# A two-block transformer in one launch: the last block's 16 attention heads run as eight pairs, and the expert rows get rings of four buffers

## The reference, cut to what matters

```python
h = modulate(rms_norm(x, norm_attn), sh1, sc1)
x = x + g1 * hybrid_mixer(h, w_in, w_out, rel_bias)      # 16 causal heads of 64
h = modulate(rms_norm(x, norm_ffn), sh2, sc2)
x = x + g2 * peer_ffn(h, peer_wq, peer_subkeys, peer_u, peer_v)
return rms_norm(x, norm_final)
```

## Time and profile before

| what | value |
|---|---|
| median of 3 runs | 2196.6 us (2193.18 to 2200.11) |
| the profiled execution | 2197.04 us, its span 2195.8 us |
| busy: TensorE / VectorE / ScalarE / GpSimd | 1870.3 / 1365.4 / 783.3 / 891.7 us |
| first scores of the heads to end of the last `out2` half | 1270.1 to 1428.5 us |
| first gather issued, last gather issued | 1468.1 us, 2170.2 us |
| gathered from the two tables | 268.47 MB on the software queue |

### The profile page before, as it was taken

The page is one execution under the profiler, slowest core; times in us unless marked ns, Lnnn a source line. Parts: engine busy times, 40 slices in busy tenths (PEclk is TensorE's granted clock), DMA queues, the critical chain, the costliest instruction groups (busy, mean ns, idle before and its releaser), DMA issues.

```text
span 2195.8 us, 29808 instructions
## 1 busy us (share of the span) xinstructions
PE 1870.3 (85%) x11372; PEld 1514.3 (69%) x11372; DVE 1365.4 (62%) x2217; ACT 783.3 (36%) x1235; POOL 891.7 (41%) x858
## 2 busy tenths in 40 slices
PE   7999978999899988778999888878777777777786
PEld 7999967999899987668999776676333233333332
DVE  6766764765476455657664574268878886444444
ACT  5443343543344334444443354332322323111111
POOL 5511630002552365340005012025566776677774
PEclk9999998999999999989999898789988988999999
DMA  7775634555566554334556244148899999999996
GB/s 237 220 274 183 205 112 140 167 191 198 176 212 201 196 162 156 130 106 136 173 199 202 80 141 144 49 133 326 325 390 384 404 389 381 375 410 409 410 410 275
DMA packets 248228, 516.47 MB, mean 235 GB/s; under 512 B 16017, under 2 KB 157634, under 8 KB 248130
## 3 DMA queue, kind: packets, MB, share of 16 engines
q0 software_dynamic: 83280, 302.06, 36.4%
q1 hardware_dynamic: 164178, 211.92, 28.9%
q10 hardware_dynamic: 672, 1.18, 0.2%
HBM read 509.86 MB, written 5.26 MB: 235 GB/s over the span
## 4 chain that ended last, share of the span: by engine, by line
PE 31%; POOL 24%; issue 23%; DVE 13%; DMA 5%; ACT 4%; POOLq 0%; ACTq 0%; SPq 0%; DVEq 0%
POOL GU L566 8%; POOL GV L566 8%; PE PX L593 5%; PE PX L594 5%; PE PX L595 5%; PE P L593 3%; PE P L594 3%; PE P L595 3%; POOL adaW L486 3%; DVE WL L1393 2%; DMA adaW<-in_w_ada 2%; DVE GU L1922 2%; ACT WH L1031 2%; POOL adaW L488 2%; DMA GU<-in_peer_u,M 2%
## 5 line engine op out<-in xcount | busy, mean ns | idle before, releaser
L966 PE MATMUL P<-GV,M 128*128 128x512 f32 x1024 | 516.0, 663 | 155.7 <-ACT M L1331 140.8
L593 PE MATMUL PX<-hTh,WH 128*128 128x256 f32 x1928 | 559.0, 290 | 34.3 <-DVE WL L1393 15.5
L594 PE MATMUL PX<-hTl,WH 128*128 128x256 f32 x1928 | 552.2, 286 | 0.0
L595 PE MATMUL PX<-hTh,WL 128*128 128x256 f32 x1928 | 551.9, 286 | 0.0
L966 PEld LDWEIGHTS P<-GV,M 128*128 128x128 f32 x1024 | 212.1, 212 | 454.3 <-issue 325.3
L1393 DVE TENSOR_TENSOR WL<-WR,WH 128x2048 fp32r<-128x2048 f32 x134 | 319.5, 2385 | 265.9 <-ACT WH L1031 265.7
L1922 DVE CUSTOM_DVE_ANT_0 GU<-GU,PX 128x1024 f32<-128x1024 f32 x256 | 297.4, 1218 | 205.1 <-DMA GU<-in_peer_u,M 185.6
L593 PEld LDWEIGHTS PX<-hTh,WH 128*128 128x128 f32 x1928 | 377.1, 196 | 42.4 <-DVE WL L1393 21.1
L1031 ACT ACTIVATE WH<-WR 128x2048 fp32r<-128x2048 f32 x134 | 255.8, 1909 | 350.8 <-PE P L595 191.3
L594 PEld LDWEIGHTS PX<-hTl,WH 128*128 128x128 f32 x1928 | 377.3, 196 | 0.9 <-issue 0.7
L595 PEld LDWEIGHTS PX<-hTh,WL 128*128 128x128 f32 x1928 | 376.9, 195 | 0.0
(11 more groups left out here) (279 smaller groups left out, 2266.3 us busy)
## 6 DMA issues: line engine op xcount, KB each, us to landing
WR<-in_ffn_w_up SPq DMA_DIRECT2D x88, 1024.0 KB, 7.5
WR<-in_ffn_w_down SPq DMA_DIRECT2D x44, 1024.0 KB, 6.5
adaW<-in_w_ada POOLq DMA_DIRECT2D x48, 512.0 KB, 4.9
WR<-in_diff_w_in SPq DMA_DIRECT2D x14, 1024.0 KB, 6.4
WR<-in_w_in SPq DMA_DIRECT2D x13, 1024.0 KB, 6.8
WR<-in_mem_w_kv SPq DMA_DIRECT2D x8, 1024.0 KB, 7.2
WR<-in_peer_wq SPq DMA_DIRECT2D x8, 1024.0 KB, 8.9
WR<-in_pool_w_in SPq DMA_DIRECT2D x6, 1024.0 KB, 6.5
```

The source lines that it names most:

```text
L593: mm(o, wh, xh, start=first, stop=False, skip_group_check=skip)
L594: mm(o, wh, xl, start=False, stop=False, skip_group_check=skip)
L595: return mm(o, wl, xh, start=False, stop=last, skip_group_check=skip)
L966: last = mm(P[2 * t + q][:], diag[:, g, i], GV[:, g, i, q * 512:q * 512 + 512], start=first and i == 0, stop=False, skip_group_check=True)
```

## The change

In the attention of the last block two heads form a pair. A pair's scores leave out keys 128 to 255 of the first query tile, which the mask hides: per head 128 + 256 = 384 columns in place of 512 (`W2`), 768 for the pair. Logits, maxima, exponentials, scaling and the copy of the transposes work on 768 columns per pair; there are six transposes in place of eight, and the second v product has 128 columns. `topk` reads only the first 128 keys for the first tile. The `in2` projections move to the PSUM banks P0 and P1, the pairs use P4 to P7 and start each turn with their v product. Turns 0 to 3 carry two `in2` halves each, turn 4 one; turns 5, 6 and 8 an `out2` half. Scores of pairs 0 to 7 wait until the projections that they need are copied (`bank_free`).

In the expert stage groups 0 to 5 use two buffers and later groups four: the two added ones lie where weights and splits lay, so group 6's u rows wait until all `wq` halves are used. GpSimd's order becomes u(n+1) before v(n). The last group's v rows have a semaphore each. The g2 row is built ahead of group 6 and not between the tiles; tile 0's final sum is done during tile 1; the closing matmuls with zeros (line 998) go.

```diff
-    OUT2_SLOTS = {11: 0, 12: 1, 15: 2}
+    IN2_SLOTS = {0: [5, 6], 1: [7, 8], 2: [9, 10], 3: [11, 12], 4: [13]}
+    OUT2_SLOTS = {5: 0, 6: 1, 8: 2}
...
+        def gather_u(n):
+            call = ALL_CALLS.index((n // GROUPS, n % GROUPS * NG // 16))
+            pool.wait_ge(S["index_ready"], call + 1)
+            if user_before(n) is not None:
+                pool.wait_ge(S["dots_ready"], user_before(n) + 1)
+            if n == EARLY:
+                pool.wait_ge(S["half_used"], len(half_of))
+            gathers(rows_u(n), ub, [u_landed[ring(n)]] * NG, n)
+
+        def gather_v(n):
+            if user_before(n) is not None:
+                pool.wait_ge(S["v_used"], user_before(n) + 1)
+            gathers(rows_v(n), vb, last_landed if n == 2 * GROUPS - 1 else [v_landed[ring(n)]] * NG, n)
...
+        gather_u(0)
+        for n in range(2 * GROUPS):
+            if n + 1 < 2 * GROUPS:
+                gather_u(n + 1)
+            gather_v(n)
...
+        def pair_scores(i):
+            a = ATT["moba"] + i
+            pe.wait_ge(S["logits_ready"], a)
+            pe.wait_ge(S["bank_free"], p["E"] + 4 + 3 * (i // 2))
+            for c in range(2):
+                r = slice(64 * c, 64 * c + 64)
+                for t, cols_of_t in enumerate(PAIR_SUM):
+                    last = mm(P[4 + c][:, cols_of_t], hQ[r, i, t * 128:t * 128 + 128], hK[r, i, 0:128 + 128 * t], start=True, stop=True)
+            last.then_inc(S["score_done"], 1)
...
+        pair_scores(0)
+        for i in range(PAIRS + 1):
+            if i + 1 < PAIRS:
+                pair_scores(i + 1)
+            if i >= 1:
+                pair_weighted(i - 1)
+            for j in IN2_SLOTS.get(i, []):
+                half("in2", j)
             if i in OUT2_SLOTS:
...
+            if i < PAIRS:
+                pair_transposes(i)
+        out2_half(3)
...
+            nc.scalar.activation(PTP[:, a % 2], PXF[:, 1024:1024 + 2 * W2], copy).then_inc(S["pt_ready"], 1)
```

More of the change, by code:

```diff
@@ L38 @@
 NG = 4
+EARLY = 6
 GROUPS = 128 // NG
@@ L332, in heads_of @@
                          bias=bias1[:, h % 2], bias_sem=(S["bias_ready"], h + 1), split=False, head=h) for h in range(8)]
[L333 to L340, removed]
+    PAIRS = 8
+    PAIR_SUM = [slice(0, 128), slice(128, W2)]
     ADA = {}
@@ L912, in _ @@
         pe.wait_ge(S["idx_relu"], 4)
-        pe.wait_ge(S["bank_free"], p["E"] + 5)
-        def dense_in2(i):
-            if i in IN2_SLOTS:
-                half("in2", IN2_SLOTS[i])
-            if i in OUT2_SLOTS:
-                v = OUT2_SLOTS[i]
-                pe.wait_ge(S["o_ready"], ATT["moba"] + (4 * v + 4 if v else IN2_LAST + 2))
-                rows_half(phases["out2"]["U"] + v, 2 * v, v == 0, False)
-        units = heads_of("heads")
-        for h in (4, 8, 12):
-            units[h]["need"] = p["E"] + 4 + 3 * (h // 4)
@@ new lines, in pair_transposes @@
+        def pair_transposes(i):
+            a = ATT["moba"] + i
+            pe.wait_ge(S["prob_ready"], a + 1)
+            pe.wait_ge(S["pt_ready"], a)
+            pe.wait_ge(S["o_ready"], a)
+            for c in range(2):
+                for t in range(2):
+                    nc.tensor.transpose(P[6][:, c * T + t * 128:c * T + t * 128 + 128], LBP[:, a % 2, c, 128 * t:128 * t + 128], ident[:])
+                last = nc.tensor.transpose(P[7][:, c * 128:c * 128 + 128], LBP[:, a % 2, c, T:T + 128], ident[:])
+            last.then_inc(S["tr_done"], 1)
@@ L1361, in _, with variance @@
         last.then_inc(S["g2_diag"], 1)
+        rows_out(1)
         act.wait_ge(S["g2_tr"], 1)
         for q in range(2):
-            last = nc.scalar.activation(g2bc[:, q * 512:q * 512 + 512], P[6 + q][:], copy)
+            last = nc.scalar.activation(g2bc[:, q * 512:q * 512 + 512], P[4 + q][:], copy)
         last.then_inc(S["g2_ready"], 1)
-        with act.Fori(0, GROUPS // 2) as r:
-            for g in range(2):
-                experts(1, r, g)
-        for t in range(2):
+        act.wait_ge(S["g2_ready"], 1)
+        for q in range(2):
+            nc.scalar.activation(P[4 + q][:], htok1[:, q * 512:q * 512 + 512], copy).then_inc(S["htok_moved"], 1)
+        def variance(t):
             act.wait_ge(S["xf_ready"], t + 1)
@@ L1374, in _ @@
                 .then_inc(S["fstd_ready"], 1)
+        for n in range(EARLY, GROUPS + 8):
+            experts(n)
+            if n in CALL_AT:
+                gate_exps(CALL_AT[n])
+            if n == GROUPS + 3:
+                variance(0)
+        with act.Fori(0, GROUPS // 4 - 2) as r:
+            for n in range(GROUPS + 8, GROUPS + 12):
+                experts(n, r)
+        variance(1)
     @block.vector
```

370 lines of the change are left out of this document (219 added, 151 removed).

## The result

The changed kernel took 2137.0 us (median of 4 runs, 2135.5 to 2142.6) beside 2198.4 us of the kernel before (4 runs): a ratio of 0.972, 95% interval 0.970 to 0.975. Forecast were 2136 us. The profiled execution is the longest of the four, 2142.6 us, its span 2141.4.

A forecast was written before the change was run, and what follows sets the result against it. TensorE bound the heads' first half, the engine-to-engine round of a head its second; gather transfers paced tile 1, stalls slowed tile 0. Gains of 29 (heads), 31 (experts) and 0.5 us (end), 60.5 together, gave 2136 us, range 2118 to 2166.

The forecast's parts named there:

- Work 104.3: Heads' stage: TensorE's work, 76.8 us for 13 projection halves plus 27.5 for the pairs, at the upper clock level.
- A pair costs ... 3.82: Heads' stage, TensorE per pair: six transposes 0.80, v products 1.5, scores 1.52, together 3.82 us.
- (a): Heads' stage, turns 2 to 6: v product waits for ScalarE's copy of the transposes, 0.7 us a turn, 3.5 together.
- (b): Heads' stage, turn 1: scores of pair 2 wait for half 6's copy, behind half 8's split on VectorE, 4.3 us.
- (c): Heads' stage, turn 5: `out2` needs the copy of half 13, of which TensorE's work leaves 0.6 us uncovered.
- (d): Heads' stage, turn 7: v product 2.2 us late, then pair 7's transposes wait 2.8 us for split, scaling and results.
- (e): Heads' stage, turn 8: TensorE waits 1.1 us for a copy.
- Start 0.6: Start of the heads' stage: scores of pair 1 wait 0.6 us for the logits of pair 0.
- Clock 8: Heads' stage: lower TensorE clock for some work behind (b), (d) and at the start, costing 8 us.
- Experts: 31.5 forecast with the end: Experts' stage: 31 us gained from removed stalls and issuing one batch ahead, less small losses; 0.5 us at the end.
- The faster one: Experts' rival: with rings of four, transfers follow GpSimd's issue pace, 422 GB/s, 17 us more gain, 2119 us; chance 0.06.
- The slower one: Heads' rival: TensorE stays at 1.2 GHz through the pairs, costing 96 us, total 2233 us; chance 0.03.

The follow-up runs named there:

- first setting: Runs of the first result: the kernel before took 2198.4 us, the changed kernel 2137.0 us, ratio 0.972.
- second setting: All later runs, what differs is not known: the kernel before took about 2260 us, the changed kernel again 2249.3 us, ratio 0.993.
- braked: Changed kernel with its buffers and issue order, but gathers of group n wait for dot products and matmuls of n-2: 2212.3 us, ratio 0.979.

## Why the prediction was right, step by step

The median came within 1 us of the forecast; the terms did not, and part of the agreement is luck. Against the profiled execution the forecast of 2136.5 is 6.1 us too low: the heads gained 3.2 us more than forecast, the experts 9.2 less. The other three executions are 5.5 to 7.2 us shorter than the profiled one, and no trace shows where.

**Heads' stage: 127.4 forecast, 123.8 measured.** All waits but the one at the start stood where they were expected, but one cost left out that two heads overlap, and the sizes were off both ways: work 11 us less, waits and start 9 more, clock 1.5 less.
- Work 104.3: too much by 11. A half takes 5.81 (11.61 for the two of turn 2), 13 of them 75.5, not 76.8. "A pair costs ... 3.82" is the step that failed: measured are 0.75, 0.93 and 0.80, together 2.48. I scaled by columns what the earlier trace rows show for one head (1.01 and 1.00 for 512), but the two heads of a pair lie in different row halves (scores) or column halves (v products) of the array and run side by side; shown by 1.57 and 1.5 us where they don't. TensorEngine Tiling (Array Packing) of the Trainium skill, Key Properties, says that different tiles can run matmuls in parallel; the traces agree (0.93 against 1.57 us, 0.80 against 1.5).
- Waits 14.5: measured 18.1. (a) five times 1.18, not 0.7: the scores of 0.93 cover less of ScalarE's work than 1.52 would have. (b) 4.36 for 4.3. (c) 1.78 for 0.6. (d) 2.04 and 3.11 for 2.2 and 2.8. (e) 0.90 for 1.1.
- Start 0.6: measured 5.7 (1272.15 to 1277.88, the scores of pair 1 in it), the largest miss among the waits. I looked for the logits of pair 0 and not for what stands ahead of them on VectorE: the split of half 6, which waits for ScalarE, and the copy of half 4. A wait of 4.9 us for the logits is the result.
- Clock 8: what is left, 123.8 less 93.5 of work, 18.1 and 5.7, is 6.5 us, in which small gaps are counted too.

**Experts: 31.5 forecast with the end, 22.3 measured.** Up to group 6 it went as written: its u rows 73.7 us behind the first gather (72.9 forecast), then 409 to 410 GB/s without a gap, with GpSimd's waits for the matmuls down from 51.5 to 10.1 us. VectorE kept up in tile 0 (268.4 us busy in the stretch of 320). The end went as written too, if it is read from the last landing. Forecast was that TensorE starts on the last two groups 5.1 us ahead of the last landing and ends 9.2 behind it. The last gather was issued at 2098.27 and landed 24.4 us later, at 2122.7; the matmuls ran from 2117.81 to 2131.78, from 4.9 ahead of it to 9.1 behind. The gain at the end is about none, as forecast.

So the whole miss lies ahead of the last landing: 686.7 us from the first gather to it, where the forecast leaves 677.5 (708.5 before, less 31). Most of it is a term that the sum put at nothing: the sixteen transfer engines don't finish together. Until 2114 the share is 1.03, but the last landing comes 8.7 us later, and at the end the share is 0.06, one engine of sixteen. Before, with few gathers outstanding, the transfers ran out in 2 us (last landing 2177.0):

```profile
2174.00:2175.00 1.00, 1.00 (x3) 0.38 (x2) 1.00 (x3) 0.00 (x0) 0.00 (x0) 1.00 0.97 385
2176.00:2177.00 1.00, 1.00 (x4) 0.32 (x2) 0.70 (x2) 0.18 (x1) 0.00 (x0) 1.00 0.03 12
```

The difference, some 6 to 7 us, is an estimate from these shares. It is also why the v rows of group 62, issued 10 us ahead of those of 63, were complete only at 2117.7: their last part lay with the late engine. DMA: Bandwidth & Descriptors of the Trainium skill, Latency and other measured facts, says that two of the sixteen engines are usually slower; the shares here fit two at 2117 to 2119 (0.11) and one at the end.

**The rivals.** The faster one fell: GpSimd did issue a gather every 1.24 us, but the transfers stayed at 409 and the queue only got longer, 24 us from issue to landing at the end. The limit of 358 GB/s that the Trainium skill states (DMA: Bandwidth & Descriptors, Where 436 GB/s comes from) did not bind in the first setting (410). The slower one had no start: the clock was 0.90 over the stage. That gathers issued far ahead might land slower stood in the prediction as a sign of error without a chance of its own. In the first setting they landed later, but the rate held. In the second setting rings of four with the new order cost about 33 us (changed against braked), though the gathers landed soon after their issue there; with it the ratio is 0.993 and not the forecast 0.972.

**Open.** What makes VectorE stand still in the second setting. Shown is that it stands still between its own instructions, more so with rings of four than with rings of two or the brake, late in GpSimd's unbroken runs, and that the kernel before has it too. Whether the gathers, the records that the later traces lose, or something outside this core is the cause isn't in the profile. How the gain of the first setting divides between the rings and the experts' other edits stays open too: no kernel but the whole change was run there, so that the rings remove the stalls of tile 0 rests on one trace (waits gone, 409 for 380 GB/s) and on no experiment.

## What to carry to other kernels

Run two heads of 64 as a pair when they lie in different halves of the array: on TensorE the second one is nearly free (0.6 us a pair less in the scores, 0.7 in the v products). Whether the whole gets shorter depends on what waits behind: without the overlap of the scores it took as long as with it. Before moving a matmul to the head of a turn, read what stands ahead of its input in the other engines' lists; copying out ahead of splitting was worth 12.9 us with its companions. A deeper ring lets the issuing engine run ahead, which cost nothing but a late last engine in one setting and 1.5% in another (braked against unbraked), so measure it in more than one setting. And when a profile names no releaser, first count whether its landing records are complete: here most were missing, and the same wait looked new only for that.

## What the runs showed of the hardware

- Two matmuls in different row halves or column halves of TensorE run side by side: 0.93 against 1.57 us and 0.80 against 1.5 us for the same columns, whichever order they are issued in.
- The same kernel, same inputs: 409 GB/s of gathers in one setting, 331 to 358 in another. There VectorE stands still between two of its own instructions, 5.9 us in one place; inside `choose` 71 us in all against 0.0.
- To issue gathers without the waits of rings of two moved fewer bytes a second there (331 and 358 GB/s against 351 and 376 in the braked kernel), with no more than 5 gathers outstanding in either.
- With 15 gathers of 512 KB outstanding on average the transfers kept 410 GB/s, but the last landing came 8.7 us after the end of the full share; with 3 outstanding on average, 2 us after it.
